# Routing the rows of a fused mixer and mixture-of-experts layer: the router's logits taken from the first sublayer's sum, block by block, with early stores and an accumulating last store

## The reference, cut to what matters

```python
out, _, _ = _token_mix(h, *mix_w, tabs, cache_ckv[:, l], cache_krope[:, l])
xs = xs + gt1 * _rmsnorm(out, g_post1[l])        # the first sublayer's sum
h = _modulate(xs, g_pre2[l], sh2, sc2)           # rmsnorm(xs, g) * (1 + scale) + shift
xs = xs + gt2 * _rmsnorm(_hier_moe(h, *moe_w), g_post2[l])
...
def _hier_moe(h, w_rg, b_rg, w_re, b_re, w_gate, w_up, w_down):
    g_prob = softmax(xt @ w_rg + b_rg);  g_top, g_idx = top_k(g_prob, 1)
    e_logits = (xt @ w_re + b_re).reshape(-1, 4, 8);  e_sel = that of the chosen group
    e_top, e_idx = top_k(softmax(e_sel), 2)
    e_w = e_top / sum(e_top) * g_top
    out = sum over experts of gates[:, e] * ((silu(xt @ w_gate[e]) * (xt @ w_up[e])) @ w_down[e])
```

## Time and profile before

| what | us |
|---|---|
| median of 3 runs | 736.13 (735.31 to 736.33) |
| the profiled execution | 733.19, span 731.4 |
| projection of five blocks and what is between (first to last L1449) | 319.1 to 391.9 |
| first gathered rows turned on TensorE | 427.0 |
| weights of pair 3 asked for | 461.7 |
| last pair's gate and up matmuls begin | 679.5 |
| last scatter issued | 694.2 |
| last instruction ends | about 731 |

### The profile page before, as it was taken

The page is one execution under the profiler, slowest core; times in us unless marked ns, Lnnn a source line. Parts: engine busy times, 40 slices in busy tenths (PEclk is TensorE's granted clock), DMA queues, the critical chain, the costliest instruction groups (busy, mean ns, idle before and its releaser), DMA issues.

```text
span 731.4 us, 8068 instructions
## 1 busy us (share of the span) xinstructions
PE 592.8 (81%) x3086; PEld 304.1 (42%) x3087; DVE 267.3 (37%) x451; ACT 147.1 (20%) x296; POOL 93.8 (13%) x102
## 2 busy tenths in 40 slices
PE   0889899999999999989999267878988777878700
PEld 0656566555555455544455223334333332322200
DVE  2316899998540244402333531101101000100137
ACT  3220000012315444402223102100110000100042
POOL 5000001500000000001110044011111111110015
PEclk9999999999999999999999769989999998999955
DMA  9999935000008510054005720799999999999273
GB/s 334 345 362 369 365 120 198 13 0 1 0 1 353 218 70 1 1 191 181 30 29 228 289 69 30 278 413 405 423 425 424 423 426 427 425 426 407 99 307 144
DMA packets 48548, 169.15 MB, mean 231 GB/s; under 512 B 5642, under 2 KB 14187, under 8 KB 36218
## 3 DMA queue, kind: packets, MB, share of 16 engines
q1 hardware_dynamic: 41216, 156.11, 53.7%
q0 software_dynamic: 6016, 10.96, 4.2%
q10 hardware_dynamic: 1274, 1.52, 0.6%
HBM read 161.48 MB, written 14.44 MB: 241 GB/s over the span
## 4 chain that ended last, share of the span: by engine, by line
PE 59%; DMA 21%; DVE 7%; issue 5%; ACT 3%; PEldq 1%; PEld 1%; DVEq 1%; SPq 1%; ACTq 1%; POOLq 0%
DMA arena<-in_w_up 14%; PE ps L1265 13%; PE ps L1449 9%; PE ps L1502 9%; PE ps L1424 5%; PE ps L1270 4%; PE ps L1515 4%; PE ps L1266 4%; DMA arena<-in_w_ada 3%; PE ps L1433 3%; PE ps L1283 2%; DVE arena L1249 2%; PE ps L1349 2%; DMA x<-in_x_sample 2%; PE ps L1403 1%
## 5 line engine op out<-in xcount | busy, mean ns | idle before, releaser
L1502 PE MATMUL ps<-arena 128*64 128x512 f32 x544 | 129.3, 628 | 22.5 <-DMA arena<-in_w_up 18.0
L1265 PE MATMUL ps<-arena 128*128 128x512 f32 x256 | 131.4, 595 | 1.2 <-issue 1.2
L984 DVE SCALAR_TENSOR_TENSOR arena<-arena 128x655 f32<-128x655 f32 x116 | 95.0, 897 | 0.4 <-issue 0.2
L1502 PEld LDWEIGHTS ps<-arena 128*64 128x64 f32 x544 | 45.5, 145 | 105.1 <-issue 97.2
L1270 PE MATMUL ps<-cst,arena 128*128 128x128 f32 (+2 forms) x349 | 54.7, 300 | 33.0 <-DVE arena L923 17.5
L1515 PE MATMUL ps<-arena 128*64 128x512 f32 x272 | 64.1, 614 | 16.4 <-ACT arena L862 15.8
L1266 PEld LDWEIGHTS ps<-arena 128*128 128x128 f32 x256 | 48.6, 190 | 61.2 <-issue 61.2
L1449 PE MATMUL ps<-arena 128*128 128x512 f32 x160 | 69.2, 593 | 0.9 <-ACT arena L814 0.9
L1270 PEld LDWEIGHTS ps<-cst,arena 128*128 128x128 f32 (+2 forms) x349 | 45.1, 179 | 51.3 <-issue 41.1
L1207 DVE TENSOR_TENSOR arena<-arena,ps 128x256 f32<-128x256 f32 x16 | 6.7, 422 | 132.0 <-ACT arena L867 119.1
L1212 DVE COPY arena<-ps 128x1024 f32<-128x1024 f32 x16 | 19.6, 1225 | 92.6 <-PE ps L1515 92.6
(11 more groups left out here) (239 smaller groups left out, 523.7 us busy)
## 6 DMA issues: line engine op xcount, KB each, us to landing
arena<-in_w_gate SPq DMA_DIRECT2D x16, 2048.0 KB, 19.8
arena<-in_w_up SPq DMA_DIRECT2D x16, 2048.0 KB, 26.0
arena<-in_w_down SPq DMA_DIRECT2D x16, 2048.0 KB, 30.7
arena<-in_w_ada SPq DMA_DIRECT2D x12, 2048.0 KB, 14.1
arena<-y_d SPq DMA_DIRECT2D x10, 512.0 KB, 7.0
arena<-in_w_in SPq DMA_DIRECT2D x8, 512.0 KB, 13.0
arena<-in_w_out SPq DMA_DIRECT2D x1, 4096.0 KB, 12.9
arena<-ada_d SPq DMA_DIRECT2D x8, 512.0 KB, 10.5
```

Source lines behind the costliest of these rows:

```text
L984: ins = dve.scalar_tensor_tensor(dst, src, w, dst, ALU.mult, ALU.add)
L1265: mm(pp(name)[:, 0:TS], lhs(k), rhs_s(k), start=k == 0, stop=k == steps - 1)
L1502: last = mm(ps[a:a + ROWS, s, :], src[:, k, a:a + ROWS], slots[w][:, j, 0:2, k * FE:(k + 1) * FE], start=k == 0, stop=k == KD - 1)
```

## The change

Seven parts:

1. The router's logits no longer come from the turned h2. Since h2 = x·r·a2 + b2 with r the row's inverse root mean square, TensorE turns x itself, multiplies it by router weights that were multiplied by a2 beforehand (`wr0` for context, `wr` for latent rows), and VectorE multiplies by r and adds a bias row (weights times b2 plus bias). For that a group `turn34` turns four modulation rows and a group `rb` multiplies the router's weights by b2, both in the middle part; GpSimd scales the weights; two tiny matmuls spread the bias over the partitions into `bias_ps` (group `small`) right before P0. The router's weights are loaded in another layout: runs of 16 and 128 bytes in place of 128 bytes and 1 KB.
2. The choice of group and experts runs per block (`route`), the places per block (`places` on TensorE, `find` on VectorE) and the table is summed up per block (`table`), at fixed points within the matmuls of the next blocks' projection.
3. For the last block the projection goes by halves, so that squares and products of the first half run beside the second.
4. x is stored to the outputs early, block by block, behind each store of h2. At the end GpSimd issues DMAs that add the second share to the outputs in DRAM; the adds on GpSimd and VectorE are gone.
5. The down weights of pairs 1 and 2 are asked for after the second gather has landed; gate and up of pair 2 when P4 is done, as before. The gather for pair 3 goes out before the first scatter.
6. For the last pair the gate matmuls wait only for the gate weights, the up matmuls for the up weights; the last copy is halved between VectorE and ScalarE.
7. ScalarE takes epsilon as its bias, so that two small VectorE operations per row block fall away, in both norms.

TensorE's list around the projection:

```diff
+            begin(pe, "small")
+            pe.wait_ge(wr2_ready, 1)
+            for v in range(2):
+                last = mm(bias_ps[:, v, :], ones[0:G + E, :], diag[:, v, :], start=True, stop=True)
+            last.then_inc(bias_in, 1)
             pe.wait_ge(wo_in, 16)
-            pe.wait_ge(wr_ready, 1)
+            pe.wait_ge(bias_ready, 1)
...
+            for b in range(NT):
+                name = f"P{b}"
...
+                for n, (k, half) in enumerate(steps):
+                    if b == 0 and k == 0:
+                        pe.wait_ge(mixc_ready, CM)
+                    if b >= 2 and n == 2:
+                        pe.wait_ge(place_ready, b - 1)
+                        table(0, b - 2)
+                    if b and n == 6:
+                        turn_rows(b - 1)
+                    if b and n == 9:
+                        logits(b - 1)
+                    if b and n == 15:
+                        places(b - 1)
+                    last = mm(pp(name)[:, half * 512:(half + 1) * 512], mixT[:, k, b * P:(b + 1) * P],
+                              wo[:, k, half * 512:(half + 1) * 512], start=k == CM, stop=k == CM - 1)
...
+            turn_rows(NT - 1)
+            pe.wait_ge(place_ready, NT - 1)
+            table(0, NT - 2)
+            logits(NT - 1)
+            places(NT - 1)
+            pe.wait_ge(place_ready, NT)
+            table(0, NT - 1)
```

VectorE (`find(b)` waits for the places of block b, forms two one-hot masks and gives `place_ready`):

```diff
             dve.wait_ge(gg1_in, 32)
             dve.wait_ge(a2_in, 32)
             dve.wait_ge(b2_in, 32)
+            dve.wait_ge(bias_in, 1)
+            dve.tensor_copy(biasrow, bias_ps).then_inc(bias_ready, 1)
...
+            for b in range(NT - 1):
+                v = min(b, 1)
+                name = f"P{b}"
+                dve.wait_ge(pss, b + 1)
+                dve.tensor_tensor(po[:], pp(name), gg1[:, v, :], ALU.mult)
+                dve.wait_ge(psd, b + 1)
+                step(dve.reciprocal(stat[:, 5, b:b + 1], stat[:, 5, b:b + 1]))
+                free(dve.scalar_tensor_tensor(x[:, b, :], po[:], stat[:, 5, b:b + 1], x[:, b, :], ALU.mult, ALU.add), name)
+                dve.drain().then_inc(x1_ready, 1)
+                if b:
+                    find(b - 1)
+                dve.wait_ge(xsd, b + 1)
+                step(dve.reciprocal(stat[:, 7, b:b + 1], stat[:, 7, b:b + 1]))
+                if b >= 2:
+                    dve.wait_ge(h2_st[b % 2], 16 * (b // 2))
+                dve.scalar_tensor_tensor(h2[:, b % 2, :], x[:, b, :], stat[:, 7, b:b + 1], a2[:, v, :], ALU.mult, ALU.mult).then_inc(h2m_ready, 1)
...
+                route(b)
+            find(NT - 2)
```

The functions that these lists call:

```diff
+            def turn_rows(b):
...
+                begin(pe, f"ht{b}")
+                pe.wait_ge(x1_ready, b + 1)
+                for k in range(KD):
+                    if b == NT - 1 and k == KD // 2:
+                        last.then_inc(t_half, 1)
+                        pe.wait_ge(x1_ready, NT + 1)
+                    last = turn(pp(f"ht{b}")[:, k * P:(k + 1) * P], x[:, b, k * P:(k + 1) * P])
...
+            def logits(b):
...
+                for k in range(KD):
+                    if b == NT - 1 and k == KD // 2:
+                        emptied(pe, f"ht{b}")
+                    last = mm(lg_ps[:, b, :], x1T[:, k, :], (wr if b else wr0)[:, k, :], start=k == 0, stop=k == KD - 1)
+                last.then_inc(lg_done, 1)
...
+            def places(b):
...
+                pe.wait_ge(mask_ready, b + 1)
+                steps = [(trib if a == b else onesb, c, a) for a in range(b + 1) for c in range(2)]
...
+            def table(n, b):
...
+                pe.wait_ge(number_ready, b + 1)
...
+            def first_best(out, v, hit, best, rank, then=1.0):
...
+                step(dve.reduce_max(best, v, AX.X))
+                step(dve.scalar_tensor_tensor(hit, v, best, rank, ALU.is_equal, ALU.mult))
+                step(dve.reduce_max(top[:, 0:1], hit, AX.X))
+                step(dve.tensor_scalar(out, hit, top[:, 0:1], then, ALU.is_equal, ALU.mult))
...
+            def route(b):
...
+                dve.wait_ge(lg_done, b + 1)
+                step(dve.scalar_tensor_tensor(L, lg_ps[:, b, :], stat[:, 7, b:b + 1], biasrow[:, v, :], ALU.mult, ALU.add))
+                first_best(pen, Lg, hitg, best0, rankg, 1e30)
...
+                first_best(oh[:, 0, b, :], em, hit, best1, ranke)
+                step(dve.scalar_tensor_tensor(em, oh[:, 0, b, :], -2e30, em, ALU.mult, ALU.add))
+                first_best(oh[:, 1, b, :], em, hit, best2, ranke)
+                dve.tensor_scalar(rt_e[:, b, 0:G], Lg, best0, None, ALU.subtract).then_inc(mask_ready, 1)
...
+            def find(b):
...
+                dve.wait_ge(pos_done, b + 1)
+                for c in range(2):
+                    dve.scalar_tensor_tensor(junk[:, c, :], pos_ps[:, b, :], 1.0, oh[:, c, b, :], ALU.mult, ALU.mult, accum_out=at[:, c, b:b + 1])
+                dve.drain()
+                for c in range(2):
+                    last = dve.tensor_scalar(place1[:, c, b, :], iota, at[:, c, b:b + 1], None, ALU.is_equal)
+                last.then_inc(place_ready, 1)
```

The stores at the end and the loads:

```diff
+            gp.wait_ge(x_st, 16 * NT)
+            for b in range(NT):
                 gp.wait_ge(f_norm, b + 1)
-                gp.tensor_tensor(x[:, b, :], x[:, b, :], yo[:, b % 2, :], ALU.add).then_inc(f_out[0], 1)
+                gp.dma_start(out_rows(b), yo[:, b, :], accum_op=ALU.add).then_inc(out_st, 16)
...
-            load_pair(2, 2)
-            sp.wait_ge(h2_last, 1)
+            load_pair(2, 2, pieces=range(2))
+            sp.wait_ge(h2_ready, NT)
+            sp.wait_ge(xg_in[1], 16)
             load_pair(1, 1, pieces=range(2, 3))
+            load_pair(2, 2, pieces=range(2, 3))
+            sp.wait_ge(x1_ready, NT + 1)
+            sp.dma_start(out_rows(NT - 1), x[:, NT - 1, :]).then_inc(x_st, 16)
...
+            emptied(pe, "turn34")
+            pe.wait_ge(wr_ready, 1)
+            begin(pe, "rb")
+            for k in range(KD):
+                last = mm(pp("rb")[0:G + E, 0:2], wr[:, k, :], b2T[:, k, :], start=k == 0, stop=k == KD - 1)
+            done(last, "rb")
...
-            act.dma_start(x_rg, i["w_rg"][0].rearrange("(p k) e -> p k e", k=KD)).then_inc(wr_in, 16)
-            act.dma_start(x_re, i["w_re"][0].rearrange("(p k) e -> p k e", k=KD)).then_inc(wr_in, 16)
+            act.dma_start(x_rg, i["w_rg"][0].rearrange("(k p) e -> p k e", p=P)).then_inc(wr_in, 16)
+            act.dma_start(x_re, i["w_re"][0].rearrange("(k p) e -> p k e", p=P)).then_inc(wr_in, 16)
```

More of the change, by code:

```diff
@@ L135, in hybrid_layer @@
     order = pe_groups()
-    place = {name: (n % 4, n // 4) for n, name in enumerate(order)}
+    homes = [HOME.get(name, n % 4) for n, name in enumerate(order)]
+    place = {name: (homes[n], homes[:n].count(homes[n])) for n, name in enumerate(order)}
     with ExitStack() as ctx:
@@ L749, in _ @@
             act.drain().then_inc(cachekv_ready, 1)
+            landed(act, "rb")
+            free(act.activation(lgb[:], pp("rb")[0:G + E, 0:2], ACT.Identity, bias=rbias[:]), "rb")
             landed(act, "krdup")
@@ new lines, in _ @@
+            b = NT - 1
+            name = f"P{b}"
+            act.wait_ge(p_half, 1)
+            squares(pp(name)[:, 0:512], stat[:, 0, b:b + 1], pss, NT, po)
+            numbers(b - 1)
+            landed(act, name)
+            squares(pp(name)[:, 512:], stat[:, 3, b:b + 1], pss, NT + 1)
+            act.wait_ge(rest_ready, 1)
+            act.activation(stat[:, 5, b:b + 1], stat[:, 3, b:b + 1], ACT.Sqrt, bias=stat[:, 1, b:b + 1], scale=1.0 / D).then_inc(psd, 1)
+            act.wait_ge(x1_ready, NT)
@@ new lines, in _ @@
+            find(NT - 2)
+            b = NT - 1
+            name = f"P{b}"
+            dve.wait_ge(pss, NT + 1)
+            dve.tensor_tensor(po[:, 512:], pp(name)[:, 512:], gg1[:, 1, 512:], ALU.mult)
+            dve.wait_ge(psd, NT)
+            step(dve.reciprocal(stat[:, 5, b:b + 1], stat[:, 5, b:b + 1]))
+            for half in range(2):
+                part_ = slice(512 * half, 512 * (half + 1))
+                ins = dve.scalar_tensor_tensor(x[:, b, part_], po[:, part_], stat[:, 5, b:b + 1], x[:, b, part_], ALU.mult, ALU.add)
+                if half:
+                    free(ins, name)
+                    dve.drain().then_inc(x1_ready, 1)
+                else:
+                    ins.then_inc(x1_ready, 1)
@@ L1184, in _ @@
             step(dve.tensor_scalar(extra[:, 0:PAIRS], extra[:, 0:PAIRS], ROWS.bit_length() - 1, None, ALU.arith_shift_right))
-            runs = [rt[0:1, 8, 2 * n * PAIRS:2 * (n + 1) * PAIRS] for n in range(2)]
-            dve.memset(rt[0:1, 8, 0:4 * PAIRS], 0.0)
-            step(None)
+            for run in runs:
+                last = dve.memset(run, 0.0)
+            step(last)
             step(dve.tensor_copy(runs[0][:, PAIRS:], extra[:, 0:PAIRS]))
@@ L1360, in _ @@
                 low_rank(n, name)
+                if n == 1:
+                    begin(pe, "turn34")
+                    pe.wait_ge(rows_ready, 5)
```

(26 more changed lines are left out.)

461 lines of the change are left out of this document (219 added, 242 removed).

## The result

The changed kernel takes 753.31 us (median of 4 runs, 753.07 to 753.45); the kernel before took 735.72 in the runs beside it (median of 4, 734.55 to 736.33). The ratio is 1.0243, with a 95% interval of 1.0223 to 1.0262: 17.6 us slower. The forecast was 752.5 us, 16.4 above the kernel before.

What follows compares the result with a forecast made beforehand. The expert weight stream, 218 us from pair 0's end, was taken to set the pace. Terms 4.5 + 10.5 + 9.7 + 16.2 - 15.9 - 8.6 = +16.4 on 736.1 gave 752.5 us, range 740 to 764.

Steps and rivals of the forecast that it cites:

- steps 2 and 4: TensorE waits, with clock loss: for the bias row before P0, +10.5 us; for places in P2, P3, P4, +16.2.
- Rivals A and B: A: VectorE's late signals don't stop TensorE, 725.8 us, chance 0.11. B: only the places are in time, 736.3, chance 0.05.
- C: The stops are there, but TensorE's clock holds over the 3.4 us gaps: 746.5 us, chance 0.16.
- Step 3: Router work moved between the projection's matmuls, P0 to P4: +9.7 us.
- step 5: From P4's end to the first turned rows: 19.2 us in place of 35.1, so -15.9.
- 6: The tail: earlier gate matmuls of the last pair -1.0, halved copy -0.6, last stage -7.0; -8.6 us in all.
- rival D: At the end, the accumulating stores form a queue, five at 5.8 us each: +14.2, 766.7 us, chance 0.08.
- step 1: Before the projection: turn34 and rb 2.5 us, the router weights' short pieces 2.0; +4.5 in all.
- opening: Early stretch to TensorE's last matmuls waiting for adaptive weights; short router pieces in a full DMA were to add 2.0 us.
- the moved router: Router turns, logits, places and tables put between the projection's matmuls, P0 to P4: +9.7 us.
- the stream's end: Last pair's gate matmuls start once TensorE is done with pair 14, at 678.4 in place of 679.50: -1.0 us.

Runs made afterwards that it cites:

- e5: On e3, SP gives out pair 2's weights and the two down loads only once h2's last store has landed: 730.56 us, ratio 0.9932.
- e6: On e3, GpSimd's five last stores write the second share alone, without adding the first sum: 723.97 us, ratio 0.9831.
- e12: On e3, last block added by VectorE and stored plainly by SP, router's weights asked for later: 723.21 us, ratio 0.9839.
- e11: As e10, on the kernel before, but the last block is added by VectorE and stored plainly by SP: 727.67 us, ratio 0.9918.
- e10: Kernel before with only the new last stage (early stores, five places, accumulating stores; no halved copy): 730.57 us, ratio 0.9954.
- e3: Changed kernel with VectorE's bias copy ahead of three waits and TensorE's table five matmuls later: 726.52 us, ratio 0.9873.

## Why the prediction was right, and where it was not

**Right, with its mechanism:** steps 2 and 4. The stops stand where they were put, two matmuls into P2, P3 and P4 and ahead of P0, with the lengths worked out (3.12 to 3.48 for 3.4, 8.1 for 8.2) and the clock's share (2.6 for 2.3, 6.9 for 6.0). Taking each away gives it back, and the wait alone, in the kernel before, costs 9.9 us. Rivals A and B needed stops under 10.3 us in all or none for the places; C needed the clock to hold, and it fell behind each stop. Step 3 is best read where nothing stops: P0's start to P4's end takes 81.8 us in all seven profiles with both orders mended, and 72.8 in the three with neither the new router nor a wait, so the moved work is 9.0, 0.7 under the 9.7. The 8.4 of the account is a remainder and has the errors of the other terms in it.

**Right in kind, mis-sized:** step 5. Two of its terms were off (E is P4's end, as in the prediction). The logits behind P4 run at half clock (3.63 for 1.94), behind a wait of TensorE of 2.5 us for VectorE's sum; the first gather's indices (L1228) were ready at 444.28, E+15.1, where the prediction had E+13.4. And the last h2 store was given 2.6 from the earlier trace rows, with 4 MB of weights queued until E+10; it landed 7.0 after its issue, at E+15.8, 3.3 behind the E+12.5 of the prediction, and held the gather for 0.8 beyond the 0.9 that it takes behind its indices. It went out at E+16.7, where the prediction had E+14.3, and 2.0 us remained at the first turned rows. The larger part is the logits' clock, the smaller the store. The first turns to pair 3's weights, "nothing changes", took 36.9 for 34.7, with this chain of what ended last in pair 0's second round:

```profile
465.24 0.64 ACTq L942
...
466.26 5.42 another core or an unknown queue
```

L942 stands behind ScalarE's branch into a pair's further round. Nothing ties the 2.3 us to the change: the stretch is 34.7, 37.0, 34.0 and 34.4 us in the four profiles of kernels without the new router, and 33.5 to 36.9 in the ten with it. What ScalarE and VectorE wait for after that branch is open; e5 excludes the down loads.

**The term that failed** is in 6: "it is nearer to the first, since reads and writes of different rows overlap: 4.5". The accumulating store took 6.8, above the upper bound of 5.8 made of a read and a write in turn, so the last stage gave -2.9 and not -7.0. The place of that cost was right, its size was not, and rival D, a queue of stores at 5.8 each, is wrong too: five stores 1.6 to 2.9 us apart are in flight together, and the last lands 7.8 after its issue, 1.0 over the median. The Trainium skill, DMA: Bandwidth & Descriptors, section Anatomy of one DMA, gives, by its fit for a GpSimd DMA, an estimated 3.2 us for this size; e6's plain stores agree with 2.9. The accumulating store measured 2.0 to 2.3 times the plain one. VectorE's part of the stage was right: its last row comes 21.2 us after y's loading, where the prediction's times make it 21.9. The -1.0 for the last pair's gate matmuls was too little: pair 3's issue to those matmuls is 217.8 to 218.2 us in the four profiles without part 6 and 214.0 to 215.9 in the ten with it, beyond the bounds of 0 to -1.1; where the rest comes from no run shows.

**Not shown:** step 1. 2.0 us for the router's short pieces were read from one queue row of one profile. The opening scatters over 4.5 us from execution to execution of kernels that are equal in it, and the means differ by 1.1. Three times the pieces ended it at 93.3 in one profile, but by way of ScalarE's held list, and not in the times. What is shown is the rest of the step, from the opening's end to O3's start: 226.6 us in nine of the ten changed kernels (e12 has 227.4), and 225.3, 226.2, 226.1 and 225.3 in the old ones, so 0.3 to 1.3 for turn34 and rb in place of 2.5. That O3 nevertheless ended only 1.6 us later was the clock: its ten matmuls took 6.23 in the profile of before and 4.53 in that of the changed kernel.

So the mechanism was right, and that the forecast landed 0.8 us from the median was luck, because errors of opposite sign met: the last stage (+4.2) and the stretch behind P4 (+4.3 with the second round) against the opening (-2.9), the moved router (-1.3) and the stream's end (-1.0), and the traces together came out 3.9 above the sum. The medians came out only 1.2 above it, 17.6 for 16.4: the profile of before lies 2.5 us under its median and that of the changed kernel on its own, so about 2.5 of the 20.3 belong to the one execution that was profiled. The last 0.4 is the median of before, 735.7 where the forecast was added to 736.1.

## What to carry to other kernels

When work is moved into a stretch in which one engine runs without a break, its price can lie less in the work than in the order of the signals that the engine then waits for. Here the work was 9 us, and the places of two waits cost 27 us of a change that is otherwise worth 9; the same change won when VectorE's copy went ahead of three waits that it doesn't need and TensorE's use of the places went five matmuls later. Ask of each new wait which count it stands on, what comes ahead of that count in the signalling engine's list, and add the clock that an idle TensorE loses. Take a term of 2 us from more than one profile before it is believed, and replace a store at the end of a kernel by an accumulating one only where the add that it saves is longer than the 3 to 4 us that it lands later; for the last block it is not, as far as e11 against e10 tells.

## What the runs showed of the hardware that was not expected

An accumulating store of 512 KB from GpSimd lands in 5.5 to 8.6 us (medians of 5.8 to 7.5 in the eight profiles with five of them), the same store without accumulation in 2.9, and its issue occupies GpSimd for 0.85 us in place of 0.53. A plain store of SP beside accumulating ones took 4.4, 4.5 and 5.9 us in three profiles, where the median of the kernel before is 2.6. Giving out a transfer can hold the issuing engine: ScalarE's third and fourth requests of the router's weights, 1024 pieces each and only 16 and 128 KB, took 4.92 and 3.70 us behind a first and second of 0.45 and 0.60, and a request of SP for 2 MB takes 0.37 us or, in the full stream of the changed kernel, up to 10.4. A gather of 512 KB that starts beside 8 MB of weights landed in up to 10.7 us, where the first ones of the kernel before have 4.2 to 5.3 and those of e3 5.2 to 6.3; over all gathers of the kernel before, most of them in the full stream, the median is 10.0. TensorE's granted clock was at 0.50, its level of 1.2 GHz, over the first 5 us behind a stop of 7.5 us; behind stops of 3.12 and 3.48 us, eight matmuls took 5.2 to 6.6 us in place of 3.44. The length of the stop alone doesn't tell the loss: behind P4 the clock was at 0.50 from 433 to 437 after a stop of 2.50 us, while 2.90 us in the earlier trace rows cost 0.25.
